# A transformer block on one core: the first modulation by feature tiles, beside the q projection

## The reference

```python
def modulation(cvec, w_mod, b_mod):
    m = jax.nn.silu(cvec) @ w_mod + b_mod
    return jnp.split(m[:, None, :], 6, axis=-1)

sh1, sc1, g1, sh2, sc2, g2 = modulation(c, w_mod, b_mod)
csh1, csc1, ... = modulation(c_ctx[None], w_mod, b_mod)
hx = rms_norm(x, norm1_g) * (1.0 + sc1) + sh1
hc = rms_norm(ctx, norm1_g) * (1.0 + csc1) + csh1
q, k, v, u, g = split(hx @ w_in)      # q 1024, k and v 256 each, u 1024, g 2048 columns
kc, vc = split(hc @ w_in[:, 1024:1536])
```

## Time and profile before

| | us |
|---|---|
| median of 3 runs | 1117.77 |
| lowest, highest | 1116.77, 1118.16 |
| the profiled run, its own time | 1119.80 |
| its span in the profile | 1118.0 |
| PE busy | 1018.6 (91%) |
| DVE busy | 619.9 (55%) |
| ACT busy | 504.0 (45%) |
| POOL busy | 136.4 (12%) |

### The profile page before, as it was taken

How to read it: one execution, slowest core, us unless ns; L and a number is a source line. 1 busy time by engine, 2 the same in 40 slices (tenths; PEclk the granted TensorE clock), 3 DMA queues, 4 the chain that set the end, 5 groups by cost and what they waited for, 6 DMA issues and landing times.

```text
span 1118.0 us, 15950 instructions
## 1 busy us (share of the span) xinstructions
PE 1018.6 (91%) x6592; PEld 901.3 (81%) x6592; DVE 619.9 (55%) x686; ACT 504.0 (45%) x628; POOL 136.4 (12%) x157
## 2 busy tenths in 40 slices
PE   4699997689989999997999999979999799999997
PEld 1498775458869999985999998778977599999886
DVE  0585387836787666545554544463345664545445
ACT  2563244335435666432544443347633354444343
POOL 3120699500000000001000000010000100000000
PEclk9699998898989999999899999989975899999999
DMA  9755055376555556463555547534421366554621
GB/s 355 278 166 210 3 194 181 113 264 206 188 169 191 187 174 201 174 203 113 188 178 184 171 143 236 178 123 151 148 79 56 115 188 188 183 183 167 213 81 38
DMA packets 118498, 189.02 MB, mean 169 GB/s; under 512 B 3024, under 2 KB 95312, under 8 KB 115376
## 3 DMA queue, kind: packets, MB, share of 16 engines
q1 hardware_dynamic: 116624, 181.61, 48.2%
q0 software_dynamic: 1136, 4.06, 1.2%
q10 hardware_dynamic: 688, 2.63, 0.6%
HBM read 187.24 MB, written 1.05 MB: 168 GB/s over the span
## 4 chain that ended last, share of the span: by engine, by line
PE 78%; DVE 13%; ACT 3%; DMA 3%; issue 1%; POOL 1%; SPq 0%; DVEq 0%; POOLq 0%; ACTq 0%
PE acc L576 15%; PE acc L577 15%; PE acc L578 15%; PE acc L573 9%; PE acc L575 9%; PE acc L574 9%; DVE XN L1544 4%; DVE wlo L1386 3%; DMA raw<-in_w_mod 2%; ACT whi L1031 1%; PE acc L645 1%; DMA raw<-in_w_attn_out 1%; DVE XN L1400 1%; PE tp L662 1%; ACT FULL L1153 1%
## 5 line engine op out<-in xcount | busy, mean ns | idle before, releaser
L1386 DVE TENSOR_TENSOR wlo<-raw,whi 128x2048 fp32r<-128x2048 f32 x148 | 340.1, 2312 | 221.0 <-ACT whi L1031 220.7
L576 PE MATMUL acc<-x_hi,whi 128*128 128x256 f32 x1376 | 395.0, 287 | 3.8 <-DVE x_lo L1424 2.0
L577 PE MATMUL acc<-x_lo,whi 128*128 128x256 f32 x1376 | 392.7, 285 | 0.0
L578 PE MATMUL acc<-x_hi,wlo 128*128 128x256 f32 x1376 | 392.5, 285 | 0.0
L1031 ACT CAST whi<-raw 128x2048 fp32r<-128x2048 f32 x148 | 280.3, 1910 | 184.5 <-PE acc L575 90.9
L576 PEld LDWEIGHTS acc<-x_hi,whi 128*128 128x128 f32 x1376 | 267.6, 194 | 11.6 <-issue 10.0
L577 PEld LDWEIGHTS acc<-x_lo,whi 128*128 128x128 f32 x1376 | 267.7, 195 | 0.0
L578 PEld LDWEIGHTS acc<-x_hi,wlo 128*128 128x128 f32 x1376 | 267.6, 194 | 0.0
L573 PE MATMUL acc<-whi,h_hi 128*128 128x512 f32 x264 | 103.1, 391 | 0.0
L574 PE MATMUL acc<-wlo,h_hi 128*128 128x512 f32 x264 | 102.7, 389 | 0.0
L575 PE MATMUL acc<-whi,h_lo 128*128 128x512 f32 x264 | 102.7, 389 | 0.0
(11 more groups left out here) (238 smaller groups left out, 1118.5 us busy)
## 6 DMA issues: line engine op xcount, KB each, us to landing
raw<-in_w_in SPq DMA_DIRECT2D x30, 1024.0 KB, 5.5
raw<-in_w_mod SPq DMA_DIRECT2D x24, 1024.0 KB, 7.9
raw<-in_w_up SPq DMA_DIRECT2D x22, 1024.0 KB, 5.1
raw<-in_w_ffn_gate SPq DMA_DIRECT2D x22, 1024.0 KB, 5.3
raw<-in_w_ffn_up SPq DMA_DIRECT2D x22, 1024.0 KB, 5.4
raw<-in_w_ffn_down SPq DMA_DIRECT2D x22, 1024.0 KB, 5.0
raw<-in_w_down SPq DMA_DIRECT2D x11, 1024.0 KB, 5.0
raw<-in_w_out SPq DMA_DIRECT2D x8, 1024.0 KB, 5.0
```

The lines of the kernel that those rows point to most:

```text
L576: pe.matmul(out, wh, xh, start=start, stop=False)
L577: pe.matmul(out, wh, xl, start=False, stop=False)
L578: return pe.matmul(out, wl, xh, start=False, stop=stop)
L1386: dve.tensor_tensor(wlo[slot][:, :], raw[raw_slot][:, :], whi[slot][:, :], ALU.subtract)\
```

## The change

- The first block's modulation is repacked: chunk k (`early`, [128, 8 x 256]) holds, for all 1024 rows of `w_mod`, the 128 columns of the shift and the 128 of the scale of feature tile k. Four buffers `early0` to `early3` of their own hold them, beside the ring.
- `first_mod(k)` multiplies it in 8 matmuls of 256 columns; four column groups of PE hold partial sums, each over two row blocks. `first_turn(k)` adds the four up as it turns them. DVE copies (`first_row`), adds the bias and makes the gain of tile k (`first_out`); ACT makes the high part of tile k (`first_hi`), DVE the low (`first_lo`).
- q runs by feature tile: four chunks of [2 x 128 rows, 1024 columns], and all four results open at once.
- x is transposed into the `acc` banks and copied to SBUF by DVE in four copies.
- SP's order is written out; x, the rest of the constants and the context come from SP's queue.
- The context's normalization, transposes and parts are moved behind u; a u tile now stands ahead of the rope transposition of the same number; POOL takes x's roots ahead of the rotary tables.
- All chunks of the ring are packed on the host, ahead of the launch, in load order: each is 1 MB in one piece, 8 KB to a partition, where `w_in`, `w_up` and others were read in runs of 1 KB, 2 KB or 4 KB.

```diff
-STAGES = [("modA", KD, 1), ("q", 4, 4), ...
+STAGES = [("q", 4, 4), ...
...
-"q": [deep(w_in, 4 * r, 512 * b) for b in range(2) for r in range(2)],
+SOURCE = {"q": [wide("w_in", 2 * r) for r in range(4)],
...
@@ SP
+            def ring(c):
+                slot_free(c)
+                sp.dma_start(raw[c % NR][:, :], stream[c, :, :]).then_inc(landed[c % NR], 16)
+            def first_block(k):
+                if k >= 4:
+                    sp.wait_ge(s["moda_ps"], k - 3)
+                sp.dma_start(early[k % 4][:, :], a["early"][k, :, :]).then_inc(early_in[k % 4], 16)
             sp.dma_start(vt[:, :, :], a["vecs"]).then_inc(s["vec_in"], 16)
+            for t in range(TT):
+                sp.dma_start(X[:, t, :], a["x"][t * P:(t + 1) * P, :]).then_inc(s[f"x_in{t}"], 16)
+            first_block(0)
+            ring(POS["q", 0])
+            first_block(1)
+            first_block(2)
+            ring(POS["q", 1])
+            first_block(3)
+            first_block(4)
+            ring(POS["q", 2])
+            first_block(5)
+            first_block(6)
+            ring(POS["q", 3])
+            first_block(7)
+            ring(POS["u", 0])
+            sp.dma_start(consts[:, C_FIRST:C_END], ...).then_inc(s["rest_in"], 16)
+            ring(POS["u", 1])
+            sp.dma_start(CTX, ...).then_inc(s["ctx_in"], 16)
...
@@ PE
+            def first_mod(k):
+                pe.wait_ge(early_in[k % 4], 16 * (k // 4 + 1))
+                if k >= 2:
+                    pe.wait_ge(s["mod_row"], k - 1)
+                for j in range(2):
+                    for b in range(MB):
+                        r = MB * j + b
+                        mm = pe.matmul(tp[32 * b:32 * b + 32, k % 2, 0:T], sct[:, r, :],
+                                       early[k % 4][:, r * T:(r + 1) * T], start=(j == 0), stop=(j == 1))
+                mm.then_inc(s["moda_ps"], 1)
+            def first_turn(k):
+                pe.wait_ge(s["mod_row"], k + 1)
...
+            def q_tile(k):
+                chunk_ready(SPLIT["q"] + k // 2)
+                pe.wait_ge(s["x0_lo"], k + 1)
...
-            for k in range(KD):
-                if k == 4:
-                    transpose_tokens(0, XN)
-                mod_chunk("modA", k, POS["modA", k])
-            mod_turn("modA")
+            x_transposes(0)
+            first_mod(0)
+            x_transposes(1)
+            first_turn(0)
+            first_mod(1)
+            first_turn(1)
+            for k in range(2, KD - 1):
+                first_mod(k)
+                q_tile(k - 2)
+                first_turn(k)
+            first_mod(KD - 1)
+            first_turn(KD - 1)
+            q_tile(5)
+            q_tile(6)
+            q_tile(7)
...
             for j in range(4):
+                tiles_stage(SPLIT["u"] + j, ACC["u"] + j)
                 rope_transposes(j)
-                tiles_stage(SPLIT["u"] + j, ACC["u"] + j)
-            x_ready(1, 3)
-            token_stage(SPLIT["kv"], ...)
+            pe.wait_ge(s["q_t"], 4)
+            transpose_tokens(1, CTX)
+            token_stage(SPLIT["kv"], ..., x_wait=lambda x: x_ready(1, 3) if x == 2 else None)
...
@@ ACT
+            first_hi(0)
+            splits_to(1)
+            first_hi(1)
+            first_hi(2)
+            splits_to(2)
...
+            first_hi(5)
+            first_hi(6)
+            splits_to(4)
+            first_hi(7)
+            splits_to(SPLIT["u"] + 1)
...
@@ DVE
...
+            first_out(5)
+            first_row(6)
+            first_lo(5)
+            first_out(6)
+            splits_to(4)
+            first_row(7)
+            first_lo(6)
+            first_out(7)
+            first_lo(7)
+            splits_to(SPLIT["u"] + 1)
```

More of the change, by code:

```diff
@@ L224, in build @@
         modrow = sb("modrow", [P, MW])
+        ph0 = ExitStack()
+        early = [sb(f"early{i}", [P, CH], F32, ph0) for i in range(4)]
+        ph0.close()
         ph1 = ExitStack()
@@ L257, in build @@
         s = {n: ctx.enter_context(nc.semaphore(n)) for n in SEMS}
+        early_in = [ctx.enter_context(nc.semaphore(f"early_in{i}")) for i in range(4)]
         landed = [ctx.enter_context(nc.semaphore(f"landed{i}")) for i in range(NR)]
@@ L322, in build @@
-        down = [a["w_down"], a["w_ffn1_down_2"], a["w_ffn2_down_2"]]
-        for n in range(3):
-            src[f"down{n}"] = [rows(down[n], 2 * r, min(2, KF - 2 * r)) for r in range(11)]
+        stream = a["stream"]
         kind = []
@@ L330, in build @@
             block, _, k = name.partition(".")
-            if block in MOD_BLOCKS and (int(k) if k else j) == KD - 1:
+            if block in MOD_BLOCKS and int(k) == KD - 1:
                 kind.append(("acc_ready", MOD_ACC[block] + 1))
@@ new lines, in first_turn, with x_transposes @@
+            def first_turn(k):
+                pe.wait_ge(s["mod_row"], k + 1)
+                for q in range(2):
+                    mm = pe.matmul(tp[:, 2, 4 * k + 2 * q:4 * k + 2 * q + 2],
+                                   modrow[:, (k % 2) * T + q * P:(k % 2) * T + (q + 1) * P], pick_sum,
+                                   start=True, stop=True)
+                mm.then_inc(s["mod_ps"], 1)
+            def x_transposes(t):
+                pe.wait_ge(s["xn_ready"], t + 1)
+                for k in range(KD):
+                    mm = pe.transpose(acc[:, k // 2, (k % 2) * T + t * P:(k % 2) * T + (t + 1) * P],
+                                      XN[:, t, k * P:(k + 1) * P], ident)
+                    if t == TT - 1 and k % 2:
+                        mm.then_inc(s["xt_ps"], 1)
@@ new lines, in _, with first_hi @@
+            for t in range(TT):
+                act.wait_ge(s["ri_ready"], t + 1)
+                act.activation(XN[:, t, :], X[:, t, :], ACT.Identity, scale=ri[:, t:t + 1]).then_inc(s["xn_ready"], 1)
+            def first_hi(k):
+                act.wait_ge(s["affine1"], k + 1)
+                act.activation(xhi[:, k, :], FULL[:, k, :], ACT.Identity, scale=gainA[:, 0, k:k + 1],
+                               bias=modv[:, k, 0:1]).then_inc(s["x0_hi"], 1)
+            act.wait_ge(s["xt_in"], 4)
@@ new lines, in _ @@
+            first_row(0)
+            for b in range(4):
+                dve.wait_ge(s["xt_ps"], b + 1)
+                dve.tensor_copy(half(FULL, b), acc[:, b, :]).then_inc(s["xt_in"], 1)
+            dve.wait_ge(s["vec_in"], 16)
+            dve.wait_ge(s["xt_in"], 4)
+            first_out(0)
+            first_row(1)
+            first_lo(0)
+            first_out(1)
+            splits_to(1)
+            first_lo(1)
+            first_row(2)
+            first_out(2)
+            first_row(3)
@@ L1937 @@
     arrays["consts"] = constants()
+    stream = np.empty((len(STREAM), P, CH), np.float32)
+    for c, (name, j) in enumerate(STREAM):
+        w, r, k, c0, n = SOURCE[name][j]
+        stream[c] = arrays[w][r * P:(r + k) * P, c0:c0 + n].reshape(k, P, n).transpose(1, 0, 2).reshape(P, CH)
+    first = arrays["w_mod"][:, 0:2 * D].reshape(KD, P, 2, KD, P).transpose(3, 1, 0, 2, 4)
+    arrays["early"] = np.ascontiguousarray(first).reshape(KD, P, CH)
+    for w in sorted({SOURCE[name][j][0] for name, j in STREAM}):
+        del arrays[w]
+    arrays["stream"] = stream
     arrays["vecs"] = vectors(arrays)
```

287 lines of the change are left out of this document (159 added, 128 removed).

## The result

| | before | changed |
|---|---|---|
| median of 6 runs, us | 1117.76 | 1121.34 |
| lowest to highest | 1115.95 to 1118.58 | 1119.75 to 1124.44 |
| changed / before, 95% interval | | 1.0033 (1.0018 to 1.0048) |
| the profiled run, its own time | 1119.80 | 1122.39 |
| its span | 1118.0 | 1120.7 |

The forecast was 1109.4 and faster; the kernel is 3.6 us slower, 0.33% with an interval of 0.18% to 0.48%. The start went much as told, and still the time rose.

What follows compares the result with a forecast made beforehand. PE's first q product waits for the whole first block (8 MB); after the scores attention heads are DVE-bound, unchanged. 8.1 - 0.3 + 0.6 = 8.4 us gained, so 1109.4 for the median; range 1104.8 to 1115.3.

Steps and rivals of the forecast that it cites:

- Part 1: Start of the kernel: first q product moves from 43.93 to about 23.5 us, after the third modulation chunk; 20.4 gained.
- rival B: Early chain quicker: no 2 us load pause, tile 5 perhaps at high clock; 12.8 us gained, 1105.0; chance 0.12.
- Part 2: q stage: grows from 26.3 to about 38.6 us, ending at 62.1 against 70.24; net 8.1 us gained with Part 1.
- rival A: More low clock at q tile 0, u or kv, or late context parts: 1112 to 1115 us; chance 0.20.
- Part 3: End of q to the scores: 65.4 us becomes 65.7; scores start at 127.9, 7.8 us earlier.
- Part 4: Weights in load order: only the attn_out load after the last modulation chunks counts, 0.6 us gained, bounds 0 and 1.2.
- Part 5: PE goes 8 times instead of twice from full-width to 32-column products: 0.13 us a visit, within the 1.2 per modulation chunk.
- Rival C: Slower: PE stays at low clock through the q loop, q ends at 83.7, total 1131 us; chance 0.07.
- the stall: Sign before turn 7 in the q stage: PE idle some 4.5 us on DVE's copy; its absence would prove the forecast wrong.
- the loop's period: Sign in the q stage: about 4.5 us per feature tile (products, modulation chunk, turn); otherwise the forecast is wrong.

Runs made afterwards that it cites:

- start_moves: "order" with POOL's two norm-gain loads issued after the roots and the split of q chunk 0 moved earlier on ACT and DVE: 1112.15 us, 0.9947.
- order: "pad128" with ACT casting the fourth q chunk before its x_hi of tile 6, and DVE subtracting it after row 7 and x_lo of tile 6: 1112.93 us, 0.9955.
- all_moved: Kernel before with an unused 128 B tile ahead of all others, so every tile moves alike: 1117.68 us, 0.9996.
- before_wide: Kernel before with its constants tile 2 columns wider (4136 B for 4128 B), same data: 1122.28 us, 1.0034.
- unpacked: "pad128" with the stream's weight loads taken from the tensors as given, the eight early modulation tiles still packed: 1120.03 us, 1.0020.
- pad128: Changed kernel with its constants tile 30 columns wider, later tiles at the same address modulo 128 as in the kernel before: 1119.80 us, 1.0015.
- pad256: Changed kernel with its constants tile 62 columns wider, later tiles at the same address modulo 256 as in the kernel before: 1115.41 us, 0.9968.
- before_packed: Kernel before with its weights packed in load order in DRAM, in its own chunk order: 1114.22 us, 0.9973.

## Why the prediction was wrong

The step that failed is the sentence ahead of the sum: "what the change is worth is the shift of that 135.68, plus one load at 240.43". It costed what the change does to the order, and put everything behind the scores at nothing, without a reason, but for that load. Measured there: 8.1 us lost, 5.1 of them in the down stages by the tiles' addresses. By its steps:

**Part 1, the first product at 23.5: 24.84.** The chain was right, one link not: x was to have landed whole at 7.6, and its second half came at 10.57, behind a pause that I had seen in the earlier trace rows and kept for rival B. "start_moves" shows that the two small loads of POOL make it. POOL issues them at 1.6 and 2.4 us in the kernel before and in the changed one. 1.3 us lost.

**Part 2, the q stage.** The period is 4.29 us (38.69 to 42.98) for my 4.5, as the chunk kept its 1.07 and needed no 1.2: 0.8 better over four. Tile 0 ran at the low clock, 0.43 apart (turn 2 at 30.10, 5.26 after the first product, for 2.75): 2.5 worse. That was in rival A, and happened. The stall before turn 7, told as 4.5 on DVE's copy, is 4.53 on DVE's copy; "order" took it away by the two moves that the prediction's reading names. The stall's chain was 0.3 shorter, and tile 5 was low only in its first half: 0.9 better. q ended at 63.9, told 62.1.

**Part 3, q to scores: 66.3 for 65.7.** u's wait is 1.57 for 1.4, kv's 0.48 for 1.05. The 1.7 us that it gave for the low clock behind kv's old wait belong to the one trace: "all_moved" and "before_wide" have that wait of 2.07 too, and 1.00 for PEclk in 96:104.4. Parts 1 to 3 together: the scores at 130.22 for 127.9, 5.46 us of gain for 7.8.

**Part 4, packing: 0.6 told, -0.3 here.** The first cast of attn_out went from 249.41 to 244.27, a lead of 5.14 behind one of 5.46. The term itself was about right: packing took 0.68 off the wait for this load ("unpacked" against "pad128") and 0.99 in the order of before. What was missed is that in the new order the same unpacked load lands 10.0 us after its issue, where it took 9.0; why was not tried. Both the 0.68 and the 0.99 are inside the bounds of 0 and 1.2 of this term.

**Part 5, alternating shapes: 0.13 a visit at most.** The chunks took 1.07 us between full-width products (at 39.12 in the timeline above), for 1.06 of a lone one before: alternating costs nothing to be seen here.

**What no step held.** 5.1 us in the down stages, by addresses: shown by "before_wide" (the cost without the change) and "pad256" (the change without the cost). And some 2.7 us where low stretches of the clock fell otherwise at 258, 332, 735 and 858 us. That is what the two traces show; no experiment set it apart, and its cause is open. For chance speaks that "all_moved" differs from before by 6.0 us of span in just this way while their medians agree. Against it speaks that "pad256" falls short in its median too (3.0 for 8.4), and that between 125 and 300 us the four traces in the order of before have 23.9 or 30.7 us at the low level, the ten in the changed order 27.3 to 35.5. With 5.1 and 2.7 put back, 1121.3 becomes 1113.5, inside the range and in rival A's band; it would be there for low clock behind the scores, and rival A's was ahead of them.

Rival C, the only slower one, did not happen: the clock rose at 30 us and stayed high to the stall. The kernel is slower by another way. Both signs that were to prove the prediction wrong, the loop's period and the stall, came out as told; they tested the start alone. The range of 10.5 us held all I could name about the order, and no term for memory layout, though the diff showed `C_END` at 1034 for 1032.

## What to carry to other kernels

Read a diff for what it does to the allocator, not only to the order: two columns in a small tile moved every later tile by 32 B and cost 5.1 us, nearly all of the 5.46 by which the changed kernel led at the scores. When a stage that no edit touched runs longer with no idle in it, compare the pitch of its instructions and then the addresses of their operands, and test with an unused tile of padding; it is the cheapest experiment there is. A stall that a blind reading of the order can place is worth undoing in the same change: two moved lines gave 6.9 us. And before a difference of a few us between two traces is explained, look at the spread of the runs of one kernel: 8 us in "all_moved".

## What the runs showed of the hardware

- Float32 products with the activation loaded (128x128) and 512 columns of weights streaming start every 0.2267 us where the two tiles' addresses are equal modulo 256, every 0.2333 with the activation 32 B or 64 B further on (or 32 B less, -32), every 0.2324 with 128. Moving both alike changes nothing ("all_moved").
- With the weights loaded and 256 columns of the activation streaming it is the other way round: 0.1200 us with equal addresses, 0.1198 with 96 apart (`cvt_hi` in "pad128"), 0.1187 to 0.1190 with 128, 0.1180 to 0.1183 with 64 or -32, 0.1167 with +32. All at the full granted clock.
- With every start at a multiple of 32 B, the distance between the two tiles is worth up to 2.9% of a product's pitch in these runs (0.2333 for 0.2267 us).
- Two broadcast loads of 64 KB each, issued by POOL at 1.6 and 2.4 us, made a pause of some 2 us in all other loads from 5.7 us on; issued at 9.1 and 9.9 us they made one from 13.2 to 14.8 ("start_moves").
- The time at the low level of the clock in one stretch differed between kernels with the same instructions there: PEclk is 0.84 in 240:272 before, 0.79 changed, 0.95 in "before_packed" and "all_moved". It differed between the runs of one kernel too: a mean of 0.938 to 0.945 in "all_moved", with times from 1121.81 down to 1113.81.
- An idle of 2.07 us ahead of the second kv chunk was followed by the low level in two traces in the order of before (PEclk 0.80 in 96:104.4 in before and "before_packed") and not in the other two (1.00 in "all_moved" and "before_wide").
